# Down projection as seven block products with weight sums made on GpSimd, in a one-core decoder layer on Trainium2

## The chip, the core and the metric

The kernel is one launch on one of the eight cores of a Trainium2 chip. The metric is device time in microseconds (us), from launch to end, as the median of runs. Engines are named PE (TensorE), DVE (VectorE), ACT (ScalarE), POOL (GpSimd) and SP (SyncE, which here only issues DMAs).

## The reference, cut to what matters

The program computes one layer of a hybrid decoder: input projection, two kinds of attention over a prompt of 1024 tokens and 8 sampled tokens, output projection, and then a gated feed-forward part with a causal convolution of width 3. Only the last part is touched:

```python
h = _rmsnorm(x, pre_g)
g = h @ w_gate                    # (1032, 1024) @ (1024, 2816)
u = h @ w_up
gp = jnp.concatenate([prev.astype(g.dtype), g], axis=1)
c = conv_b
for j in range(CONV_W):
    c = c + conv_w[j] * gp[:, j:j + S]
a = jax.nn.gelu(c, approximate=True) * u
out = a @ w_down                  # (1032, 2816) @ (2816, 1024)
return x + _rmsnorm(out, post_g), gp[:, -(CONV_W - 1):]
```

## The kernel before

`TOK` = 1032 tokens (1024 + 8), `D` = 1024, `FF` = 2816 = `FC` = 22 blocks of `P` = 128. Every float32 operand of a product is split into a high part, written in the matmul's own format by ACT, and a low part (raw minus high) by DVE; a product is then three matmuls: high by high, high by low, low by high. Activations are kept transposed, features on the partitions and tokens along the free axis.

**Gate and up (`strassen`, blocks f = `PLAIN` = 3 to 21).** For each block of 128 gate and 128 up features, the product of a 2 x 2 split of the weights (gate or up, by two halves of the 1024 rows) with a 2 x 2 split of the tokens and rows (`HALF` = 516 tokens) is made from seven block products instead of eight. Each of the seven, `product(f, 0..6)`, is 4 x 3 x 2 = 24 matmuls of 258 tokens (`PART`), 168 in a block. Four sums of weight blocks (`sums`) are made by DVE as soon as the weights have landed. Results leave PSUM by ACT (`p1`, gate) and by DVE (`combine`: U2, U3, UP2, UP1, GATE2), and PE waits for several of these: product 3 for U2, product 5 for U3, product 6 for UP2. DVE's list in block f is: GATE2 of f-1, the four weight sums for f+1, the convolution of f-1 (one half), U2 of f, the other half of the convolution, one low part (1024 columns) for f+1, `multiply(f-1)` (the activation a of f-1 is then complete, in `cbuf`), the second low part (1536 columns), U3, the third low part (1024), UP2, UP1. Blocks 0 to 2 are made plainly, beside sums over tokens (`token_sums`) that DVE needs several long operations for.

SP's list in block f: wait for `multiply(f-1)`, store a (516 KB) to `a_dram`; wait for product 2, load the gate weights of block f+2 (512 KB); wait for product 5, load the up weights of f+2. POOL only copies ten columns of each gate block (`tail`).

**Down (`down(s)`, 88 steps).** The output (8 blocks d of 128 features, by 1032 tokens) is made in thirds of 344 tokens: sub-stages 0 and 1 (22 steps of 8 blocks), then the last third as 2 and 3 (22 steps of 4 blocks each). Each step loads a block row of `w_down` and, up to the last third, a third of a, splits both on ACT and DVE two steps ahead (`LAG`), and gives 3 matmuls of 344 tokens for each block. At the end of a sub-stage the banks are copied to `acc`. From step 46 on, tiles t of 128 tokens are turned on PE (`turn`), squared on ACT, given a root on POOL, scaled by DVE (`norm`), added to the residual by POOL (tiles below `EARLY` = 5) and stored. The remaining four tiles follow the last matmul; they use `scaled` columns and one DVE operation each.

What sets the order: every engine's list is written out by hand in one program order, and semaphores tie the lists together. The lines that the steps below use:

```python
def multiply(f):
    c = cbuf[:, f % 2, :]
    dve.wait_ge(gelu_done, f + 1)
    up_ready(dve, f)
    dve.tensor_tensor(c, c, ubuf[:, f % 2, :], ALU.mult).then_inc(mul_done, 1)
```

## Time and profile before

| | |
|---|---|
| runs | 1487.51 us median of 3 (1486.86 to 1490.24) |
| the profiled execution | 1485.53 us, its span 1483.8 us |
| PE busy | 1427.2 us (96%) |
| DVE, ACT, POOL busy | 865.6, 639.1, 365.8 us |
| gate and up by seven products, in the chain that ends last | 370.36 us of PE |
| down | 1211.9 to 1471.7 us |
| after the last matmul of down | 12.1 us |

The span is what the engines' records cover; 1.7 us of the execution lie outside it. PE runs without a gap from 841.5 us to the end of gate and up at 1211.9 us, and nearly so through down. A busy share of other engines says little here; what counts is when each link of a chain between them is done, compared with the time at which PE wants it. Those times are in the timeline rows further down.

### The profile page before, as it was taken

The numbers are of one execution on the slowest core, as the hardware profiler recorded it, in microseconds if no ns is written. First come the engines' busy times: TensorE is split into PE (matmuls) and PEld (weight loads), VectorE is DVE, ScalarE is ACT, GpSimd is POOL, SyncE is SP. The second block draws the span as 40 slices with busy tenths as digits, with TensorE's granted clock in tenths as the row PEclk, the third lists the DMA queues.
The fourth block names the chain that finished last, engine by engine and source line by source line (L and its number), as shares of the span: only waits on it lengthen the run. The fifth ranks groups of instructions, "written<-read, shape, count | busy, mean of one in ns | idle before, by whom it ended". The sixth has DMA issues, their size and how long they took to land. (4 is left out here: it accounts for less than half of the span.)

```text
span 1483.8 us, 26782 instructions
## 1 busy us (share of the span) xinstructions
PE 1427.2 (96%) x10372; PEld 1287.8 (87%) x10372; DVE 865.6 (58%) x1379; ACT 639.1 (43%) x1198; POOL 365.8 (25%) x549
## 2 busy tenths in 40 slices
PE   7999999999999899789999999999999999999998
PEld 6999777777777676477889999999999999999998
DVE  6422577667465555555439866766667755444674
ACT  6733555544455454433324523333233334433543
POOL 5223876756555541041100000000000000000120
PEclk9999999999999999999999999999999999999999
DMA  5113556777666564422321222222222246655773
GB/s 186 51 41 92 158 182 215 223 222 248 234 214 196 166 202 156 156 72 86 101 80 58 86 86 75 84 69 76 86 86 73 71 147 204 204 183 185 230 261 113
DMA packets 174840, 209.91 MB, mean 141 GB/s; under 512 B 22051, under 2 KB 118891, under 8 KB 174676
## 3 DMA queue, kind: packets, MB, share of 16 engines
q1 hardware_dynamic: 174714, 208.21, 44.5%
q8 instruction: 82, 1.34, 0.4%
q14 instruction: 44, 0.36, 0.1%
HBM read 178.37 MB, written 29.88 MB: 140 GB/s over the span
## 5 line engine op out<-in xcount | busy, mean ns | idle before, releaser
L632 POOL TENSOR_TENSOR k_page<-k_page,q_bc 128x256 f32<-128x256 f32 x256 | 183.4, 749 | 148.3 <-DMA k_page<-in_cache_fox_k 109.9
L1228 PE MATMUL PS<-ht_hi,w_hi 128*128 128x344 f32 x576 | 195.5, 339 | 6.7 <-POOL w_lo L602 4.7
L1228 PE MATMUL PS<-ht_hi,w_lo 128*128 128x344 f32 x576 | 186.4, 324 | 0.0
L1228 PE MATMUL PS<-ht_lo,w_hi 128*128 128x344 f32 x576 | 186.0, 323 | 0.0
L2466 PE MATMUL PS<-act_hi,wd_hi 128*128 128x344 f32 x528 | 169.0, 320 | 3.2 <-DVE act_lo L2301 3.2
L2466 PE MATMUL PS<-act_hi,wd_lo 128*128 128x344 f32 x528 | 168.6, 319 | 0.0
L2466 PE MATMUL PS<-act_lo,wd_hi 128*128 128x344 f32 x528 | 168.4, 319 | 0.0
L2298 DVE TENSOR_TENSOR wd_lo<-wd_raw,wd_hi 128x1024 fp32r<-128x1024 f32 (+1 forms) x88 | 87.8, 999 | 112.4 <-ACT act_hi L2109 92.4
L851 ACT ACTIVATE probs<-probs,stat 128x256 f32<-128x256 f32 (+7 forms) x128 | 98.5, 771 | 96.5 <-DVE stat L1101 95.9
L1228 PEld LDWEIGHTS PS<-ht_hi,w_hi 128*128 128x128 f32 x576 | 110.2, 191 | 32.7 <-issue 20.4
L2106 ACT ACTIVATE wd_hi<-wd_raw 128x1024 fp32r<-128x1024 f32 (+1 forms) x88 | 74.2, 845 | 139.9 <-DMA act_raw<-a_dram 103.7
L2421 PE MATMUL PS<-ht_hi,wgu_hi 128*128 128x258 f32 x608 | 122.6, 283 | 0.0
L2421 PE MATMUL PS<-ht_hi,wgu_lo 128*128 128x258 f32 x608 | 122.5, 283 | 0.0
L2421 PE MATMUL PS<-ht_lo,wgu_hi 128*128 128x258 f32 x608 | 122.5, 283 | 0.0
L2092 ACT ACTIVATE conv<-gate,conv_consts 128x1032 f32<-128x1032 f32 x22 | 27.6, 1254 | 207.4 <-DVE gate L2263 197.4
L2069 POOL COPY gate_tails<-gate 128x10 f32<-128x10 f32 x22 | 5.1, 230 | 438.2 <-DVE gate L2263 392.0
L1228 PEld LDWEIGHTS PS<-ht_lo,w_hi 128*128 128x128 f32 x576 | 110.2, 191 | 0.0
L1228 PEld LDWEIGHTS PS<-ht_hi,w_lo 128*128 128x128 f32 x576 | 110.0, 191 | 0.0
L2466 PEld LDWEIGHTS PS<-act_hi,wd_hi 128*128 128x128 f32 x528 | 99.2, 188 | 4.3 <-DVE act_lo L2301 4.2
L1025 DVE TENSOR_REDUCE scores<-k_page 128x16 f32<-128x1024 f32 x64 | 77.5, 1211 | 39.6 <-POOL k_page L632 39.4
L2466 PEld LDWEIGHTS PS<-act_lo,wd_hi 128*128 128x128 f32 x528 | 99.3, 188 | 0.0
L2466 PEld LDWEIGHTS PS<-act_hi,wd_lo 128*128 128x128 f32 x528 | 99.0, 188 | 0.0
(282 smaller groups left out, 3293.2 us busy)
## 6 DMA issues: line engine op xcount, KB each, us to landing
wd_raw<-in_w_down SPq DMA_DIRECT2D x44, 512.0 KB, 3.5
k_page<-in_cache_diff_k SPq DMA_DIRECT2D x64, 256.0 KB, 2.9
k_page<-in_cache_fox_k SPq DMA_DIRECT2D x64, 256.0 KB, 3.4
v_page<-in_cache_diff_v SPq DMA_DIRECT2D x64, 256.0 KB, 2.8
v_page<-in_cache_fox_v SPq DMA_DIRECT2D x64, 256.0 KB, 3.3
w_raw<-in_w_in SPq DMA_DIRECT2D x24, 512.0 KB, 4.9
a_dram<-conv SPq DMA_DIRECT2D x22, 516.0 KB, 3.1
act_raw<-a_dram SPq DMA_DIRECT2D x66, 172.0 KB, 3.7
```

The source lines that it names most:

```text
L632: ins = pool.tensor_tensor(kpage[:, g % 2, c:c + PIECE], kpage[:, g % 2, c:c + PIECE], qbc[:, c:c + PIECE], ALU.mult)
L851: act.activation(p, p, ACT.Exp, bias=stat[:, J % 8, m:m + 1], scale=-1.0, accum_out=stat[:, J % 8, 2 + m:3 + m]).then_inc(exp_done, 1)
L1025: dve.tensor_reduce(scores[:, b % 3, :, n, :], kpage[:, g % 2, :].rearrange("p (k m c) -> p k m c", k=2, c=HD), AX, ALU.add).then_inc(red_ ...
L1228: ins = pe.matmul(PS[:, z_bank(c), 0:THIRD], b[:, k, :], a[:, k, third(i)], start=(k == 0 and p == 0), stop=(k == KC - 1 and p == 2))
L2069: pool.tensor_copy(tails[:, f, :], gb[:, f % 2, SEQ:SEQ + DB + 2]).then_inc(tail_done, 1)
L2092: act.activation(cbuf[:, f % 2, :], gb[:, f % 2, 2:2 + TOK], ACT.Identity, bias=bias[:, f:f + 1], scale=taps[2][:, f:f + 1]).then_inc(c_in ...
L2106: act.activation(wd_hi[s % NW][:, c], wd_raw[s % NW][:, c], ACT.Copy).then_inc(down_high, 1)
L2298: dve.tensor_tensor(wd_lo[s % NW][:, c], wd_raw[s % NW][:, c], wd_hi[s % NW][:, c].bitcast(F32), ALU.subtract).then_inc(down_low, 1)
L2421: ins = pe.matmul(PS[:, bank + piece, 0:PART], w[:, k, :], a[:, k, piece * PART:(piece + 1) * PART], start=first and k == 0 and m == 0, st ...
L2466: ins = pe.matmul(PS[:, cell_bank(p, d), 0:THIRD], w[:, c], a[:, :], start=f == 0 and m == 0, stop=f == LAST and m == 2, skip_group_check= ...
```

## The change

The gate/up part keeps its products. The down product is now also made by a 2 x 2 split: 2 x 2 over (22 feature blocks in `NP` = 11 pairs) and (output features in halves of 512, tokens in halves of 516), with seven products in place of eight. `RUNS` = 9 runs of 11 steps: runs 0 to 4 are the products 0 to 4, a step being 4 output blocks x 3 x 2 = 24 matmuls of 258 tokens; products 5 and 6 are each made in two runs of half the tokens, 12 matmuls a step, so that the first tiles can be turned while the rest is still being made. Together 7 x 11 x 24 = 1848 matmuls.

The seven products need sums of operands. **Right sums** (of the activation a, four per pair of blocks): POOL makes them in `cbuf` after `multiply`, one behind even blocks and three behind odd ones, and SP stores seven halves (258 KB each, for 516 tokens) per pair to `b_dram`. **Weight sums** (`left_sums`): 44 chunks (256 KB), each a 128-column slice of four blocks of `w_down`. SP loads a chunk, POOL makes four dependent sums of 128 columns, SP stores the chunk to `s_dram`. Three chunks belong to each of blocks 4 to 17 and two to block 18, in two buffers. Down then loads whole left and right operands from `w_down`, `s_dram` and `b_dram`: 22 places for weights in place of 5, four for activations in place of 22. Finished products are added to the corners of the output by DVE as they leave PSUM; the fourth product is copied by ACT and added behind the first steps of run 4 (`add_fourth`). `EARLY` is 6, and POOL's residual add is cut in four.

```diff
+    NP = FC // 2
+    NW, NB = 22, 4
+    CHUNKS = 3
+    b_dram = nc.dram_tensor("b_dram", (7, NP, P, HALF), F32).ap()
+    s_dram = nc.dram_tensor("s_dram", (4, NP, P, WIDE), F32).ap()
+    chunks_of = lambda f: range(max(0, CHUNKS * (f - PLAIN - 1)), min(4 * NP, CHUNKS * max(0, f - PLAIN)))
...
+    FULL = 5
+    RUNS = FULL + 4
+    STEPS = RUNS * NP
+    LEFT = [(None, 0, 0), (0, 0, 0), (1, 0, 0), (3, 0, 0), (2, 0, 0), (None, 1, 1), (None, 1, 0)]
+    run_of = lambda s: s // NP
+    k_of = lambda s: s % NP
+    product_of = lambda r: r if r < FULL else FULL + (r - FULL) % 2
+    pieces_of = lambda r: (0, 1) if r < FULL else ((r - FULL) // 2,)
+    C11, C12, C21, C22 = range(4)
+    TARGET = [C11, C12, C21, C22, C12, C21, C11, C21, C11]
+    SOURCE = [None, C11, C12, C21, C12, C21, C11, C21, C11]
...
-                sp.dma_start(a_dram[f], cbuf[:, f % 2, :]).then_inc(a_stored[f % 2], 16)
+                if f % 2 == 0:
+                    store_half(f, 0, second_half)
+                else:
+                    store_half(f, 4, first_half)
+                    store_half(f, 6, second_half)
+
+            def store_sums(f):
+                k = f // 2
+                if f % 2 == 0:
+                    sp.wait_ge(pair_step, 4 * k + 1)
+                    store_half(f, 3, second_half)
+                else:
+                    sp.wait_ge(pair_step, 4 * k + 2)
+                    store_half(f - 1, 2, first_half)
+                    sp.wait_ge(pair_step, 4 * k + 3)
+                    store_half(f - 1, 1, second_half)
+
+            def store_last_sum(f):
+                sp.wait_ge(pair_step, 4 * (f // 2) + 4)
+                store_half(f, 5, second_half)
+
+            def load_chunk(c):
+                k, q = c // 4, c % 4
+                for i in range(2):
+                    src = io["w_down"][(2 * k + i) * P:(2 * k + i + 1) * P, :].rearrange("p (j c) -> p j c", j=2)[:, :, q * P:(q + 1) * P]
+                    sp.dma_start(chunk[c % CHUNKS % 2][:, 2 * i:2 * i + 2], src).then_inc(s_in, 16)
+
+            def store_chunk(c):
+                k, q = c // 4, c % 4
+                sp.wait_ge(sum_done, SUM_BASE + 4 * c + 4)
+                sp.dma_start(s_dram[:, k, :, q * P:(q + 1) * P].rearrange("m p c -> p m c"), chunk[c % CHUNKS % 2]).then_inc(s_stored, 16)
 
...
+                sums = chunks_of(f)
+                for c in sums[:2]:
+                    if c % CHUNKS == 0 and c:
+                        sp.wait_ge(s_stored, S_BASE + 16 * c)
+                    load_chunk(c)
                 if f:
-                    store_a(f - 1)
+                    store_act(f - 1)
                 if f + 2 < FC:
-                    for up in range(2):
-                        weights_free(sp, f, up)
-                        load_weights(sp, f + 2, up)
-            for s in range(2, STEPS):
+                    weights_free(sp, f, 0)
+                    load_weights(sp, f + 2, 0)
+                for c in sums[:1]:
+                    store_chunk(c)
+                if f:
+                    store_sums(f - 1)
+                for c in sums[2:]:
+                    sp.wait_ge(s_stored, S_BASE + 16 * (c - 1))
+                    load_chunk(c)
+                if f + 2 < FC:
+                    weights_free(sp, f, 1)
+                    load_weights(sp, f + 2, 1)
+                if f and f % 2 == 0:
+                    store_last_sum(f - 1)
+                for c in sums[1:]:
+                    store_chunk(c)
...
+            def left_sums(c):
+                a11, a21, a12, a22 = (chunk[c % CHUNKS % 2][:, m] for m in range(4))
+                n = SUM_BASE + 4 * c
+                pool.wait_ge(s_in, S_BASE + 32 * (c + (2, 1, 1)[c % CHUNKS]))
+                pool.tensor_tensor(a22, a21, a22, ALU.add).then_inc(sum_done, 1)
+                pool.wait_ge(sum_done, n + 1)
+                pool.tensor_tensor(a21, a11, a21, ALU.subtract).then_inc(sum_done, 1)
+                pool.wait_ge(sum_done, n + 2)
+                pool.tensor_tensor(a11, a22, a11, ALU.subtract).then_inc(sum_done, 1)
+                pool.wait_ge(sum_done, n + 3)
+                pool.tensor_tensor(a12, a12, a11, ALU.subtract).then_inc(sum_done, 1)
+            def right_sums(f):
+                k = f // 2
+                pool.wait_ge(mul_done, f + 1)
+                b11, b12, b21, b22 = cbuf[:, 0, second_half], cbuf[:, 0, first_half], cbuf[:, 1, second_half], cbuf[:, 1, first_half]
+                if f % 2 == 0:
+                    pool.wait_ge(a_stored[0], 16 * (4 * k + 1))
+                    pool.tensor_tensor(b11, b12, b11, ALU.subtract).then_inc(pair_step, 1)
+                else:
+                    pool.tensor_tensor(b12, b22, b12, ALU.subtract).then_inc(pair_step, 1)
+                    pool.wait_ge(a_stored[0], 16 * (4 * k + 2))
+                    pool.tensor_tensor(b11, b22, b11, ALU.subtract).then_inc(pair_step, 1)
+                    pool.wait_ge(pair_step, 4 * k + 3)
+                    pool.wait_ge(a_stored[1], 16 * (3 * k + 2))
+                    pool.tensor_tensor(b21, b11, b21, ALU.subtract).then_inc(pair_step, 1)
             for f in range(FC):
+                for c in chunks_of(f):
+                    left_sums(c)
                 tail(f)
+                right_sums(f)
...
-                    pool.tensor_tensor(out[:, u % OS, :], out[:, u % OS, :], xr[:, u % OS, :], ALU.add).then_inc(out_early, 1)
+                    for part in range(4):
+                        c = slice(part * D // 4, (part + 1) * D // 4)
+                        pool.tensor_tensor(out[:, u % OS, c], out[:, u % OS, c], xr[:, u % OS, c], ALU.add).then_inc(out_early, 1)
...
                 if f >= 2:
-                    act.wait_ge(a_stored[f % 2], 16 * (f // 2))
+                    act.wait_ge(a_stored[f % 2], 16 * (4, 3)[f % 2] * (f // 2))
+                    act.wait_ge(pair_step, 4 * (f // 2))
...
+                if s == NP:
+                    evacuate_first()
+                if s == 4 * NP:
+                    evacuate_fourth()
...
+            def evacuate(r):
+                pieces = pieces_of(r)
+                for d in range(4):
+                    src = PS[:, bank_of(r, d):bank_of(r, d) + len(pieces), 0:PART]
+                    if r == 0:
+                        if d % 2 == 0:
+                            cell_ready(dve, r, d)
+                            dve.tensor_copy(corner(C11, d), src).then_inc(cell_dve, 1)
+                        continue
+                    cell_free(dve, r - 1, d)
+                    if r == 4:
+                        dve.wait_ge(cell_dve, 10 + 2 * d + 2)
+                    cell_ready(dve, r, d)
+                    dst = corner(TARGET[r], d, pieces)
+                    if product_of(r) == 5:
+                        dve.tensor_tensor(dst, dst, src, ALU.subtract).then_inc(cell_dve, 1)
+                    else:
+                        dve.tensor_tensor(dst, corner(SOURCE[r], d, pieces), src, ALU.add).then_inc(cell_dve, 1)
+
+            def add_fourth(d):
+                p5, u3, u4 = corner(C22, d), corner(C21, d), corner(C12, d)
+                dve.wait_ge(cell_act, 2 + d + 1)
+                dve.wait_ge(cell_dve, 6 + d + 1)
+                dve.tensor_tensor(u4, u4, p5, ALU.add).then_inc(cell_dve, 1)
+                dve.wait_ge(cell_dve, 10 + 2 * d + 1)
+                dve.tensor_tensor(p5, p5, u3, ALU.add).then_inc(cell_dve, 1)
...
+                if s >= NP and run_of(s) != 4 and k_of(s) == (0 if run_of(s) < FULL else 1):
+                    evacuate(run_of(s) - 1)
+                if 4 * NP < s <= 4 * NP + 4:
+                    add_fourth(k_of(s) - 1)
+                if s >= STEPS - 4:
+                    scale(4 + s - (STEPS - 4))
...
+                for d in range(4):
+                    if k == 0:
+                        if r == 0 and d:
+                            if d == 1:
+                                pe.wait_ge(act_done, 2 * (FC - PLAIN))
+                            else:
+                                pe.wait_ge(evac_done, evacs(FC - 1, (UP1, GATE2)[d - 2]))
+                        elif r == FULL:
+                            cell_free(pe, r - 1, 1 + d // 2)
+                        elif r:
+                            cell_free(pe, r - 1, d)
+                    first = c.start
+                    for m, (w, a) in enumerate(((w_hi2[n % NW], b_hi[slot]), (w_hi2[n % NW], b_lo[slot]), (w_lo2[n % NW], b_hi[slot]))):
+                        for piece in range(len(pieces_of(r))):
+                            ins = pe.matmul(PS[:, bank_of(r, d) + piece, 0:PART], w[:, d * P:(d + 1) * P],
+                                            a[:, first + piece * PART:first + (piece + 1) * PART],
+                                            start=k == 0 and m == 0, stop=k == LAST and m == 2, skip_group_check=True)
+                    if k == LAST or d == 3:
                         ins.then_inc(down_done, 1)
```

SP, around block 6 of gate and up (`wgu_raw` is a set of gate and up weights, `conv` holds the activation a, `wd_sums` is a chunk; e_mul_done is raised by `multiply`, a_lf_in0 by POOL's weight sums, a_v_in0 by a chunk's landed store, e_pair_step by right sums). Before:

```order
L1506 DMA wgu_raw_94_10955<-in_w_gate 128x8x128 [waits e_prod_done]
L1506 DMA wgu_raw_94_10955<-in_w_up 128x8x128 [waits e_prod_done]
L2002 DMA a_dram<-conv_103_12174 128x1032 [waits e_mul_done]
L1506 DMA wgu_raw_91_10952<-in_w_gate 128x8x128 [waits e_prod_done]
L1506 DMA wgu_raw_91_10952<-in_w_up 128x8x128 [waits e_prod_done]
```

And now:

```order
L2083 DMA wd_sums_188_12259<-in_w_down 128x2x128 x2
L2054 DMA b_dram<-conv_103_12174 128x516 [waits e_mul_done]
L1507 DMA wgu_raw_94_10955<-in_w_gate 128x8x128 [waits e_prod_done]
L2088 DMA s_dram<-wd_sums_187_12258 128x4x128 [waits a_lf_in0]
L2054 DMA b_dram<-conv_103_12174 128x516 [waits e_pair_step]
L2083 DMA wd_sums_187_12258<-in_w_down 128x2x128 [waits a_v_in0]
L2083 DMA wd_sums_187_12258<-in_w_down 128x2x128
L1507 DMA wgu_raw_94_10955<-in_w_up 128x8x128 [waits e_prod_done]
L2088 DMA s_dram<-wd_sums_188_12259 128x4x128 [waits a_lf_in0]
```

Between the load of the gate weights and that of the up weights SP now stands at three other waits: for POOL's weight sums, for its right sums and for the landing of a chunk's store.

POOL in the same place. Before, it has the copies of `tail` alone (the first three in the plain blocks):

```order
L2063 MEMSET stat_12168 128x16
L2065 MEMSET gate_12173 128x2 x2
L2069 COPY gate_tails_12167<-gate_12173 128x10 [waits e_plain_evac] x3
L2069 COPY gate_tails_12167<-gate_12173 128x10 [waits e_evac_done,e_act_done] x19
L2076 TENSOR_SCALAR stat_12168<-stat_12168 128x1 [waits e_y_sq]
```

And now, for block 3's activation and the first chunk (the second and third chunk read the same):

```order
L2184 COPY gate_tails_12167<-gate_12173 128x10 [waits e_evac_done,e_act_done]
L2206 TENSOR_TENSOR conv_12174<-conv_12174 128x516 [waits e_mul_done]
L2208 TENSOR_TENSOR conv_12174<-conv_12174 128x516 [waits e_a_stored0]
L2211 TENSOR_TENSOR conv_12174<-conv_12174 128x516 [waits e_a_stored1,e_pair_step]
L2190 TENSOR_TENSOR wd_sums_12258<-wd_sums_12258 128x128 [waits a_kp_in0]
L2192 TENSOR_TENSOR wd_sums_12258<-wd_sums_12258 128x128 [waits a_lf_in0]
L2194 TENSOR_TENSOR wd_sums_12258<-wd_sums_12258 128x128 [waits a_lf_in0]
L2196 TENSOR_TENSOR wd_sums_12258<-wd_sums_12258 128x128 [waits a_lf_in0]
```

A block's chunks stand behind the right sums of the block before, which wait for that block's `multiply`.

DVE at the end of the first long stretch of down, where a bank group is emptied. Before, between sub-stages 0 and 1:

```order
L2298 TENSOR_TENSOR wd_lo_12188<-wd_raw_12193,wd_hi_12183 128x1024
L2301 TENSOR_TENSOR act_lo_12218<-act_raw_12240,act_hi_12196 128x344
L2309 COPY acc_12261<-PS 128x344 x4
L2298 TENSOR_TENSOR wd_lo_12189<-wd_raw_12194,wd_hi_12184 128x1024
L2301 TENSOR_TENSOR act_lo_12219<-act_raw_12241,act_hi_12197 128x344
```

And now, between run 4 and run 5:

```order
L2459 TENSOR_TENSOR wd_lo_12213<-wd_raw_12235,wd_hi_12191 128x512
L2460 TENSOR_TENSOR act_lo_12250<-act_raw_12254,act_hi_12246 128x258
L2459 TENSOR_TENSOR wd_lo_12214<-wd_raw_12236,wd_hi_12192 128x512
L2460 TENSOR_TENSOR act_lo_12250<-act_raw_12254,act_hi_12246 128x258
L2479 TENSOR_TENSOR acc_12260<-acc_12260,PS 128x516 x4
L2459 TENSOR_TENSOR wd_lo_12215<-wd_raw_12237,wd_hi_12193 128x512
```

The four additions of a finished product stand where copies stood, behind the low parts of the second step of the new run.

## Rows read from the trace of the kernel before

**Rows 1.** Chain that ended last, in order of time: start us, us, what.
```profile
841.55 370.36 PE PS L2421 x3072
1211.92 167.78 PE PS L2466 x1068
...
1385.24 0.87 PE PS L2483 x8
```

**Rows 2.** Busy time by stretch: down, and what follows (columns: us, PE, PEld, DVE, ACT, POOL, PEclk, DMA, GB/s).
```profile
1211.90:1471.70 259.80, 256.55 (x1647) 254.57 (x1645) 134.60 (x184) 111.18 (x180) 17.29 (x16) 1.00 0.62 203
1471.70:1483.80 12.10, 7.35 (x65) 6.51 (x64) 6.78 (x9) 4.47 (x9) 2.94 (x8) 0.92 0.34 133
```

**Rows 3.** Timeline of DVE in one gate/up block: start us, us, what, [idle before].
```profile
1010.42 0.70 DVE L2212 TENSOR_TENSOR wgu_raw<-wgu_raw 128x512 f32<-128x512 f32 x1 [0.17 <-DMA wgu_raw<-in_w_up]
...
1015.35 0.69 DVE L2263 TENSOR_TENSOR u<-PS,p 128x516 f32<-128x516 f32 x1 [0.71 <-PE PS L2421]
...
1018.50 1.23 DVE L2244 TENSOR_TENSOR conv<-conv,up 128x1032 f32<-128x1032 f32 x1
1019.65 1.75 DVE L1515 TENSOR_TENSOR wgu_lo<-wgu_raw,wgu_hi 128x1536 fp32r<-128x1536 f32 x1
1021.32 0.69 DVE L2263 TENSOR_TENSOR u<-PS,p 128x516 f32<-128x516 f32 x1
1021.93 1.22 DVE L1515 TENSOR_TENSOR wgu_lo<-wgu_raw,wgu_hi 128x1024 fp32r<-128x1024 f32 x1
1024.02 0.70 DVE L2263 TENSOR_TENSOR up<-PS,u 128x516 f32<-128x516 f32 x1 [0.87 <-PE PS L2421]
```

**Rows 4.** Timeline of SP's DMA queue in the same block.
```profile
1019.76 0.34 SPq L2002 DMA_DIRECT2D a_dram<-conv  x1
1020.15 0.44 SPq L1506 DMA_DIRECT2D wgu_raw<-in_w_gate  x1
1026.91 0.37 SPq L1506 DMA_DIRECT2D wgu_raw<-in_w_up  x1
```

**Rows 5.** DMA issues of the whole run: count, KB each, median us to landing.
```profile
a_dram<-conv SPq DMA_DIRECT2D x22, 516.0 KB, 3.1
wgu_raw<-in_w_gate SPq DMA_DIRECT2D x22, 512.0 KB, 4.6
wgu_raw<-in_w_up SPq DMA_DIRECT2D x22, 512.0 KB, 3.8
...
out_o_dk<-k_rows SPq DMA_DIRECT2D x8, 256.0 KB, 3.2
...
out_o_fk<-k_rows SPq DMA_DIRECT2D x8, 256.0 KB, 2.4
```

**Rows 6.** Groups of POOL by form: count, busy us, mean ns, idle before.
```profile
L632 POOL TENSOR_TENSOR k_page<-k_page,q_bc 128x256 f32<-128x256 f32 x256 | 183.4, 749 | 148.3 <-DMA k_page<-in_cache_fox_k 109.9 <-DMA q_bc<-qs_dram 34.4 <-PE PS L1354 4.0
...
L643 POOL TENSOR_TENSOR lf_after<-lf_four 128x56 f32<-128x56 f32 x8 | 2.4, 303 | 0.6
```

**Rows 7.** Timelines of POOL and DVE, a residual add in down.
```profile
1391.79 2.41 POOL L2083 TENSOR_TENSOR out_rows<-out_rows,x_rows 128x1024 f32<-128x1024 f32 x1 [3.62 <-DVE out_rows L2327]
...
1392.50 2.24 DVE L2298 TENSOR_TENSOR wd_lo<-wd_raw,wd_hi 128x512 fp32r<-128x512 f32 x1 [0.80 <-ACT act_hi L2109]
...
1395.09 0.68 DVE L2298 TENSOR_TENSOR wd_lo<-wd_raw,wd_hi 128x512 fp32r<-128x512 f32 x1
```

**Rows 8.** Timeline of DVE between the plain blocks and block 3.
```profile
819.49 6.74 DVE L2293 TENSOR_TENSOR t_lo<-t_raw,t_hi 128x2064 fp32r<-128x2064 f32 x3
...
834.46 0.69 DVE L2263 TENSOR_TENSOR u<-PS,p 128x516 f32<-128x516 f32 x1
```

**Rows 9.** Groups of DVE by form, in down: count, busy us, mean ns, idle before.
```profile
L2298 DVE TENSOR_TENSOR wd_lo<-wd_raw,wd_hi 128x512 fp32r<-128x512 f32 x44 | 33.9, 774 | 36.4 <-ACT wd_hi L2106 19.8 <-ACT act_hi L2109 16.4
```

**Rows 10.** Busy time by stretch around a pause of PE at 640 us.
```profile
640.00:642.20 2.20, 0.35 (x2) 0.14 (x2) 0.89 (x2) 0.91 (x3) 0.14 (x1) 1.00 0.00 0
642.20:645.40 3.20, 3.17 (x8) 2.52 (x9) 2.26 (x2) 3.20 (x4) 3.20 (x3) 0.50 0.72 175
```

More of the change, by code:

```diff
@@ L1943, in ffn, with right_free @@
+    def right_free(eng, s):
+        h = s - FULL * NP
+        if NB <= s < FULL * NP:
+            step_ready(eng, s - NB)
+        elif 0 <= h < 2 * NB:
+            step_ready(eng, min(FULL * NP - 3 + h // 2, FULL * NP - 1))
+        elif h >= 2 * NB:
+            step_ready(eng, s - 2 * NB)
+    ends_of = lambda s: 4 if k_of(s) == LAST else 1
     steps_done = lambda s: sum(ends_of(n) for n in range(s + 1))
-    loads_of = lambda s: 32 if s < 3 * FC else 16
-    down_loads = lambda s: sum(loads_of(n) for n in range(s % NW, s + 1, NW))
@@ L1959, in ffn @@
-    PAIR = [6, 4, 6, 4, 6, 4, 6, 0, 2]
+    PAIR = [6, 4, 6, 4, 6, 4, 6, 4, 6]
+    SCALED_PAIR = {6: 0, 7: 2, 8: 4}
     y_of = lambda t: PS[0:rows(t), PAIR[t]:PAIR[t] + 2, :].rearrange("p b c -> p (b c)")
-    EARLY = sum(third_of(t) < 2 for t in range(NS))
-    TAIL_STEP = 2 * FC + 1
-    turn_step = lambda t: TAIL_STEP + 2 + 4 * t
+    scaled_y = lambda t: PS[0:rows(t), SCALED_PAIR[t]:SCALED_PAIR[t] + 2, :].rearrange("p b c -> p (b c)")
+    EARLY = 6
+    TAIL_STEP = FULL * NP + 1
+    turn_step = lambda t: TAIL_STEP + (1, 8, 13, 18, 24, 30)[t]
@@ L2152, in _ @@
                 else:
[L2153 removed]
+                    high_parts(0)
                 if f:
@@ L2196, in _ @@
                         squares(t)
-            evacuate(3)
+            for d in range(2):
+                scale(d)
             for t in range(EARLY, NS):
@@ L2389, in _ @@
                         norm(t)
-            evacuate(3)
-            scale(3)
+            evacuate(RUNS - 1)
+            for d in range(2, 4):
+                scale(d)
             for t in range(EARLY, NS):
```

300 lines of the change are left out of this document (159 added, 141 removed).

## Prediction

> **What bounds the kernel now.** I read the chain that ended last first. From 841.55 to 1211.92 us it is nothing but gate/up matmuls, 370.36 us for 3072 of them, and then down matmuls, 167.78 us for 1068 [rows 1]. The table by stretch says the same of down: PE is busy for 256.55 of 259.80 us [rows 2]. So PE sets the end here, and fewer matmul columns are worth their full time, as long as nothing new makes PE wait. The pitch of a matmul is 370.36/3072 = 0.1206 us at 258 tokens and 167.78/1068 = 0.1571 us at 344. Next I read one gate/up block on DVE and SP [rows 3, 4], for what must be ready when. A block is 168 x 0.1206 = 20.25 us. Call M the end of `multiply`, 1018.50 + 1.23 = 1019.73. The up weights are asked for 7.2 us behind M (1026.91), when product 5 is done, and DVE's weight sums start as they land: in this block at 1010.42, 0.17 us after DVE was free. So that load has no slack against DVE already now. From the first weight sum to M are 9.3 us, of which 0.71 are a wait for PE, so 8.6 of work in a row. DVE's slack against PE is small: U3 is ready at 1022.0, and PE could use it when product 4 ends, shortly before 1024.0. That is 1.9 us.
>
> **Down, matmuls.** 22 x 24 x 3 = 1584 matmuls at 0.1571 are 248.8 us. Seven products are 1848 at 0.1206, 222.9 us: **-26.0**. The pitch is that of the same form in gate/up, also with two pieces on one weight block. Six tiles and half of two more are turned before the last matmul, in place of five: 16 more transposes at 0.87/8 [rows 1], +1.7. The stretch after the last matmul, 12.1 us [rows 2], loses half of its turns and one tile: -2.
> **Down, new waits.** A full step of DVE is a low part of 512 (0.68 undisturbed [rows 7]; the mean of 44 is 0.77 [rows 9]) and one of 516 (0.69), 1.4 of PE's 2.9 us. In runs 5 and 6 a step is 12 x 0.1206 = 1.45 us, and DVE has 0.68 + 0.4 (half of 0.69, with a start) = 1.1, beside additions of 0.69 and one 1.28 us norm a tile. That is nearly full, and GpSimd's cut adds each hold it for up to 0.75. I put +1 there. Between runs 4 and 5 the additions stand behind two low parts, and PE's first step needs two of them: +2. The fourth product's copies and additions: +1; the later run ends +1. Transfers are 24 matmuls of 520 KB, 180 GB/s, against 203 now [rows 2]; I charge nothing, and up to +5 if they land late. PE's 3.2 us of idle in down now go half. Sum for down: -26.0 + 1.7 - 2 + 5 - 1.6 = **-23** (-27 to -16).
>
> **Gate/up, the loop through SP.** Here the change adds waits. SP loads the up weights of block f+2 only behind (a) GpSimd's first weight sums of block f, (b) the right sums, (c) the landing of the first chunk's store. GpSimd's list puts (a) behind the right sums of f-1, and these wait for M. The next M waits for the up weights. That is a closed loop, once per block: M, right sums, weight sums, store, loads, DVE, next M. Queued behind SP's wait are the up weights; behind those stands DVE, and behind DVE's U2 and U3 stands PE.
>
> Prices. A GpSimd sum of 516 columns is not in the trace: 256 columns take 0.75 [rows 6], 1024 take 2.41 [rows 7], so 2.16 ns a column and 1.31 us; one of 128 is 0.47 (56 columns take 0.30 [rows 6]), with 0.08 between dependent ones, so a chunk is 2.2 us. A 256 KB store lands in 2.4 to 3.2 us, 516 KB in 3.1; I take 3.0, and 2.7 for the single half. Loads of 512 KB take 3.8 alone and 4.6 close behind another transfer [rows 5]; I take 4.25. Each issue costs 0.4.
>
> DVE and GpSimd get in each other's way: at 1392.50 a DVE low part of 512 columns, 0.68 otherwise, took 2.24 us and ended 0.5 us after GpSimd's add (1391.79 + 2.41) did [rows 7]. I take it that two such operations never run together. *The Trainium skill, "SBUF — State Buffer", "SBUF: two separate sides", says that a DVE operation with two SBUF inputs and a GpSimd operation that reads SBUF exclude one another, and the loser fully blocks; the trace agrees (2.24 for 0.68). By that rule the sum is the one below; without it, it is the first rival.* Beside M DVE runs its 1.75 low part until M+1.65, and a 1.22 one behind U3.
>
> - Even f (three right sums): first sum M+1.65 to 2.95; DVE's 1.22 part to 4.1; two more sums and a semaphore to 6.75; chunk to 8.95; store landed 12.0; two chunk loads and the up load issued by 12.9; landed 17.2; then 8.6 and 0.4 for meeting the third chunk's sums: next M at **26.2**.
> - Odd f (one right sum): its store landed 2.7, DVE's 1.22 part until 3.5, sum to 4.8, chunk 7.0, store 10.1, loads 11.0, landed 15.3: next M at **24.3**.
>
> Mean 25.25, against PE's 20.25: 5.0 us a block in iterations 4 to 17, 14 x 5.0 = 70; +2.5 for iteration 18 (two chunks, no third to wait for); -1.9 for the slack that is used once: **+71**. Nearest bounds: all stages at their short ends (stores 2.4, load 3.8, no collisions) give 21.4 a block, +16; stores 3.2, load 4.6 and a lost turn at the port in each block give 27, +95.
>
> **Gate/up, entry.** Between the plain blocks and block 3 DVE runs without idle (6.74 us of `t_lo` at 819.49, and U2 at 834.46 starts with no wait [rows 8]). The four right sums of the first pair push in between: 4 x 1.31 = **+5** (0 to +7). In blocks 19 to 21 nothing is added that PE would see: the right sums end at M+7, and the load waits for product 5 anyway.
>
> **Sum.** -23 + 71 + 5 = +53. Against the profiled execution 1485.5 + 53 = 1538.5; the median of the runs is 2.0 above that execution, so 1487.5 + 53 = **1540.5**.
>
> **Rivals.**
> 1. *The loop holds, the collisions cost nothing* (GpSimd and DVE mostly miss each other). Loop 23.9 and 23.3, +3.4 a block, 14 x 3.4 - 1.9 + 5 - 23 = +28: 1515. For it: outside M, DVE is idle much of a block. Against: right sums are released at M, where two low parts stand. 0.20.
> 2. *Faster.* Stores and loads at their short ends, and M reached earlier: the loop fits under PE's block. Place: SP's up load. It decides at 20.25 - 8.6 = 11.6 us from M to landed up weights; I count 15.3 to 17.2, the short ends 12.8. Gain 23 less the entry: 1470; with a loop of 21.4: 1484. For it: five blocks without chunks and loose orders elsewhere. Against: (c) alone is 2.4 to 3.2. 0.12.
> 3. *Slower still*: loop 27 or more, as twice the traffic of now lengthens every landing, or PE's clock: after 2.2 us with 0.35 busy it was granted 0.50, the 1.2 GHz level, for 3.2 us [rows 10]. The waits for U2 would be 3 to 5 us each. Half clock adds 1.6 us a block; I count it as hidden, since PE then waits for U2 again. *"TensorE: Matmul & The Clock Gate" of the Trainium skill, "HAM oscillation — how this bites in real kernels", has each tile start cold behind such a wait; here that is this 1.6 us.* If not hidden, 14 x 1.6 = +22: 1562; with the long loop 1565 to 1590. 0.15.
> 4. *No change*: a loop of 21.7 pays the gain back exactly. 0.03.
>
> **Chances.** Forecast 0.50, rivals 0.20, 0.12, 0.15, 0.03. Faster by over 0.2% (about what a measurement of this kernel can tell from no change) 0.12, within 0.03, slower 0.85. The range must take in rival 1 and the lower part of rival 3: 1500 to 1572 holds 0.5 + 0.17 + 0.12, about 8 in 10.
>
> **What would show it.** Right: blocks of about 25 us from block 5 on, alternating by about 2; DVE idle before the first weight sum, ended by the up weights, some 5 us a block; SP's issue of the up load 11 to 13 us behind M; GpSimd's 516-column sums at M stretched beyond 1.31; down 23 us shorter. Wrong: blocks of 20.25 with the up load issued at product 5, or a pitch in down above 0.1206, or DVE low parts ending late in runs 5 and 6 by more than a few us.

## The result and the profile after

The changed kernel takes 1540.57 us (median of 4 runs, 1535.76 to 1541.27), beside 1488.74 us before (4 runs, 1486.86 to 1490.24). The ratio is 1.033, 95% interval 1.031 to 1.036: slower. The profiled execution has a span of 1538.1 us.

I lay the profile of after beside that of before in four stretches. The marks are the issue of the load of `ffn_pre_g`, which no edit here moves (642.4 before, 649.8 after), the loads of `w_up` on SP's queue, the first matmul of down, and the end.

| stretch | before | after | difference | forecast |
|---|---|---|---|---|
| start to `ffn_pre_g` | 642.4 | 649.8 | +7.4 | 0 |
| second to sixth load of `w_up` (entry) | 73.40 | 77.07 | +3.7 | +5 |
| sixth to 20th (14 blocks) | 283.4 | 346.38 | +63.0 | +70 |
| 20th to the first matmul of down | 83.8 | 85.7 | +1.9 | +0.6 |
| down and tail | 271.9 | 250.2 | -21.7 | -23 |

The first line is code that the change leaves alone. In the 14 profiles of this study that mark stood between 642.4 and 650.6 us, and before happened to be the earliest. So inside the marks behind it the change moved this execution by +46.9, where I had forecast +53. The timed medians differ by 51.8. There is one profile of before, so whether its first stretch is always the shorter one is open.

SP's queue in one block, after (start us, us, what), which answers [rows 4]. M, the end of `multiply`, was at 1017.18:

```profile
1017.21 0.81 SPq L2054 DMA_DIRECT2D b_dram<-conv  x2
1018.07 0.45 SPq L1507 DMA_DIRECT2D wgu_raw<-in_w_gate  x1
1025.69 0.37 SPq L2088 DMA_DIRECT2D s_dram<-wd_sums  x1
1026.10 1.00 SPq L2054 DMA_DIRECT2D b_dram<-conv  x2
1028.03 1.21 SPq L2083 DMA_DIRECT2D wd_sums<-in_w_down  x2
1029.28 0.61 SPq L1507 DMA_DIRECT2D wgu_raw<-in_w_up  x1
```

GpSimd and DVE in the same block; the last line is the next M:

```profile
1017.26 2.74 POOL L2206 TENSOR_TENSOR conv<-conv 128x516 f32<-128x516 f32 x1 [8.88 <-DVE conv L2403]
1019.97 2.28 POOL L2208 TENSOR_TENSOR conv<-conv 128x516 f32<-128x516 f32 x1
1022.32 1.30 POOL L2211 TENSOR_TENSOR conv<-conv 128x516 f32<-128x516 f32 x1
...
1017.10 1.75 DVE L1516 TENSOR_TENSOR wgu_lo<-wgu_raw,wgu_hi 128x1536 fp32r<-128x1536 f32 x1
...
1019.37 1.71 DVE L1516 TENSOR_TENSOR wgu_lo<-wgu_raw,wgu_hi 128x1024 fp32r<-128x1024 f32 x1
...
1033.81 0.69 DVE L2371 TENSOR_TENSOR wgu_raw<-wgu_raw 128x512 f32<-128x512 f32 x1 [7.52 <-DMA wgu_raw<-in_w_up]
...
1041.08 1.23 DVE L2403 TENSOR_TENSOR conv<-conv,up 128x1032 f32<-128x1032 f32 x1
```

The load of the up weights is issued 12.1 us behind M, where it was 7.2 before. DVE stands idle for 7.52 us, ended by its landing, and reaches the next M 25.1 us after the last. SP's store of M goes out 0.03 us behind it in every block, so SP itself is never late here. In the block behind it, with one right sum, the load is issued at 1052.61 and M follows at 1065.81, 23.5 us after 1042.31. The waits of 820 to 1290 us say the same in sum (us, times, longest):

```profile
POOL conv L2204 <- DMA b_dram<-conv: 129.9, 10, 18.2
ACT conv L2240 <- DMA b_dram<-conv: 112.4, 8, 14.9
...
DVE wgu_raw L2371 <- DMA wgu_raw<-in_w_up: 96.2, 17, 8.8
...
PEld PS L2598 <- DVE u L2422: 47.1, 17, 5.2
```

Down, and what follows the last matmul (us, PE busy, PEld, DVE, ACT, POOL, PEclk, DMA, GB/s), which answer [rows 2]:

```profile
1287.90:1528.00 240.10, 233.90 (x1926) 231.59 (x1925) 139.87 (x225) 102.78 (x198) 32.27 (x40) 0.99 0.66 202
1528.00:1538.10 10.10, 4.56 (x40) 3.96 (x40) 4.80 (x7) 3.73 (x7) 2.21 (x6) 0.99 0.28 107
...
1445.00:1505.00 60.00, 55.01 (x445) 53.34 (x443) 41.34 (x69) 29.09 (x66) 22.95 (x30) 0.97 0.70 225
```

### The profile page after: what moved, and what is told of

It is laid out like the page before. It is cut to its first block and busy times, and to the rows that moved or that the text cites. A ratio compares the mean times of both kernels' runs of the same rounds, so it can differ in the third digit from the quotient of the medians.

```text
span 1538.1 us, 27932 instructions
## 1 busy us (share of the span) xinstructions
PE 1426.1 (93%) x10628; PEld 1279.1 (83%) x10628; DVE 875.0 (57%) x1417; ACT 633.3 (41%) x1216; POOL 543.5 (35%) x788
## 5 line engine op out<-in xcount | busy, mean ns | idle before, releaser
L2650 PE MATMUL PS<-act_hi,wd_hi 128*128 128x258 f32 x616 | 140.6, 286 | 6.2 <-DVE acc L2479 3.3
L2598 PE MATMUL PS<-t_hi,wgu_hi 128*128 128x258 f32 x456 | 99.3, 301 | 43.8 <-DVE u L2422 43.6
L2650 PE MATMUL PS<-act_lo,wd_hi 128*128 128x258 f32 x616 | 138.7, 283 | 0.0
L2650 PE MATMUL PS<-act_hi,wd_lo 128*128 128x258 f32 x616 | 138.6, 283 | 0.0
L2598 PEld LDWEIGHTS PS<-t_hi,wgu_hi 128*128 128x128 f32 x456 | 74.8, 200 | 48.8 <-DVE u L2422 47.1
L1513 ACT ACTIVATE wgu_hi<-wgu_raw 128x1024 fp32r<-128x1024 f32 (+1 forms) x63 | 72.2, 1182 | 84.7 <-DMA wgu_raw<-in_w_up 48.4
L2459 DVE TENSOR_TENSOR wd_lo<-wd_raw,wd_hi 128x512 fp32r<-128x512 f32 x77 | 56.1, 728 | 80.4 <-ACT act_hi L2258 80.4
```

Source lines behind the costliest of these rows:

```text
L1513: act.activation(hi[f % 2][:, a:b], part(raw, f, a, b), ACT.Copy).then_inc(gu_hi, 1)
L2459: dve.tensor_tensor(w_lo2[n % NW][:, :], w_raw2[n % NW][:, :], w_hi2[n % NW][:, :].bitcast(F32), ALU.subtract).then_inc(down_low, 1)
L2598: ins = pe.matmul(PS[:, bank + piece, 0:PART], w[:, k, :], a[:, k, piece * PART:(piece + 1) * PART], start=first and k == 0 and m == 0, st ...
L2650: ins = pe.matmul(PS[:, bank_of(r, d) + piece, 0:PART], w[:, d * P:(d + 1) * P], a[:, first + piece * PART:first + (piece + 1) * PART], st ...
```

## The experiments

The theory to be tested: a gate/up block is as long as the loop from M over right sums, chunk sums, landing and loads to the up weights and the next M. Its rival: GpSimd's work beside VectorE and the doubled traffic make blocks long by themselves. In the edits SP's list of one iteration is written in short; `right sums` is `store_sums(f - 1)`, `c0` to `c2` are the block's chunks. What each kernel gave (the timed ratio is to before on the same chip; the last three columns are from the profiles: second to sixth load of `w_up`, which the expectations also call third to sixth or seventh; mean of the 14 blocks behind them; start of down's first matmul to the end, which is 0.1 to 0.2 us more than by the chain's piece above). Before itself had a median of 1490.4 beside e1 to e5, 1490.8 beside e7 and e8, 1492.4 beside e9 and e10, 1490.5 beside e11 to e13 and 1485.0 in one run beside e14:

| kernel | us | ratio (95%) | entry | block | down |
|---|---|---|---|---|---|
| before | 1488.7 | | 73.4 | 20.24 | 272.0 |
| after | 1540.6 | 1.033 (1.031 to 1.036) | 77.1 | 24.74 | 250.4 |
| e1 up load before the landing | 1534.8 | 1.030 (1.025 to 1.035) | 77.3 | 24.30 | 250.4 |
| e2 up load before all of the chunks | 1525.9 | 1.024 (1.021 to 1.027) | 77.3 | 24.13 | 250.7 |
| e4 no chunks | 1465.8, one run | | 78.8 | 20.24 | 246.0 |
| e5 small right sums | 1516.9, one run | | 76.1 | 23.61 | 252.2 |
| e7 e2, two chunks a block | 1476.1 | 0.991 (0.989 to 0.994) | 82.2 | 20.24 | 251.2 |
| e8 e2, chunk loads behind M | 1492.7 | 1.002 (1.000 to 1.004) | 79.1 | 21.86 | 250.6 |
| e9 e7, later stores of y | 1475.8 | 0.991 (0.988 to 0.993) | 82.6 | 20.24 | 244.6 |
| e10 e9, chunks spread | 1487.6 | 0.997 (0.995 to 0.999) | 83.3 | 20.76 | 251.7 |
| e11 two chunks, order of after | 1530.6 | 1.028 (1.026 to 1.031) | 96.2 | 22.78 | 248.6 |
| e12 e7 again | 1476.5 | 0.990 (0.989 to 0.992) | 83.0 | 20.24 | 251.4 |
| e13 e9 again | 1475.7 | 0.990 (0.988 to 0.991) | 82.8 | 20.24 | 247.9 |
| e14 e7, no chunks in blocks 0 to 2 | 1472.7, one run | | 78.9 | 20.24 | 248.9 |

**e1: the up load one step earlier.**

```diff
 store_chunk(c0)
 store_sums(f - 1)
+weights_free(sp, f, 1); load_weights(sp, f + 2, 1)
 wait for the landing of c0; load_chunk(c2)
-weights_free(sp, f, 1); load_weights(sp, f + 2, 1)
```

> The load of w_up stands one step earlier on SyncE: behind the store of the first chunk and the stores of the right sums, ahead of the wait for that store's landing. Theory (the loop M, right sums, chunk sums, landing, loads, up weights, next M sets the block): the load is issued some 2.2 us sooner in a block with three right sums (M+9.9 for M+12.1) and 2.7 us sooner in the other (M+7.6 for M+10.3), so the blocks take 22.9 and 20.6 us for 25.1 and 23.3, and the kernel 1540.5 - 14 x 2.45 = about 1506 us (1500 to 1512). Rival (the blocks are long because GpSimd and VectorE slow each other and the chunk transfers load the DMA engines, whatever the order of issue): no more than 5 us, 1535 to 1541.

Measured: 1534.8 us, blocks of 24.30. Most of the saving did not come. In one block M was at 1011.19 and the load was issued at 1022.43, M+11.2 and not M+9.9; in the next, M 1036.17, it went out at 1044.78, M+8.6 and not M+7.6. In both SP was itself late: it was issuing chunk loads until 1011.71 and 1036.69, half a microsecond behind M. In the second the half of M landed later for it, and the right sum, which waits for that, started at M+4.3 in place of M+3.4. Over the blocks of e1 SP's store of M was 0.6 to 2.5 us late. That pointed at the chunk chain as a loop of its own.

**e2: nothing of the chunks ahead of the up load.**

```diff
+store_sums(f - 1)
+weights_free(sp, f, 1); load_weights(sp, f + 2, 1)
 store_chunk(c0)
-store_sums(f - 1)
 wait for the landing of c0; load_chunk(c2)
-weights_free(sp, f, 1); load_weights(sp, f + 2, 1)
```

> SyncE's order in a block becomes: store of the right sums, load of w_up, store of the first chunk, landing, the rest. Theory: nothing of the chunks is ahead of the load of w_up any more; it is issued when PE's product frees its buffer (M+7.2 in the kernel before), the block is PE's 20.25 us again, and the 65 us that the loop cost in gate/up go: 1476 us (1473 to 1482), which is also faster than the kernel before. Rival (collisions and traffic, whatever the order): 1530 to 1541. If the loop goes but the right sums in VectorE's way cost 1 to 2 us in a block, 1490 to 1505.

Measured: 1525.9 us, blocks of 24.13. From one issue of the up load to the next it is mostly near 21 and near 28 us by turns, and from M to M 22.2 to 26.2. My theory said 20.25, and its number fell. SP's queue of e2, where M was at 1009.60:

```profile
1002.37 6.54 SPq L2088 DMA_DIRECT2D s_dram<-wd_sums  x2
1010.83 2.52 SPq L2083 DMA_DIRECT2D wd_sums<-in_w_down  x4
1013.39 1.08 SPq L2054 DMA_DIRECT2D b_dram<-conv  x2
1014.52 0.46 SPq L1507 DMA_DIRECT2D wgu_raw<-in_w_gate  x1
1015.02 1.45 SPq L2054 DMA_DIRECT2D b_dram<-conv  x2
1016.51 0.49 SPq L1507 DMA_DIRECT2D wgu_raw<-in_w_up  x1
1021.27 0.37 SPq L2088 DMA_DIRECT2D s_dram<-wd_sums  x1
1025.98 1.21 SPq L2083 DMA_DIRECT2D wd_sums<-in_w_down  x2
1027.24 0.60 SPq L2054 DMA_DIRECT2D b_dram<-conv  x1
1027.88 5.82 SPq L2088 DMA_DIRECT2D s_dram<-wd_sums  x2
1035.64 2.52 SPq L2083 DMA_DIRECT2D wd_sums<-in_w_down  x4
1038.20 0.60 SPq L2054 DMA_DIRECT2D b_dram<-conv  x1
```

The up load is issued at M+6.9, as expected (in the next block, with M at 1034.40, only at M+9.4). But two things are new. SP stands in the chunk chain until 1010.83 and then issues four chunk loads of 0.6 us each, so the store of M goes out 3.8 us late. And all transfers now go out in one burst: from 1010.83 to 1016.51, 2.6 MB, and the up weights, last of them, start DVE only at 1025.32, 8.8 us after their issue:

```profile
1025.32 0.69 DVE L2371 TENSOR_TENSOR wgu_raw<-wgu_raw 128x512 f32<-128x512 f32 x1 [5.69 <-DMA wgu_raw<-in_w_up]
```

The chunk chain is a second closed loop: M, its store, right sums, c0's sums, store, landing, c2's load and sums, store, landing, four loads, and only then SP's store of the next M. Once around, from the store of one M (1013.39) to the store of the next (1038.20), it takes 24.8 us, and that is the length of this block from M to M (24.80), where PE needs 20.25. SP's store is 3.8 to 7.1 us late in all but the first block with chunks. The two loops are not apart in e2: SP's lateness also puts the up load at the end of the burst. They are told apart below, by e11 and e10.

**e4 and e5: one half of GpSimd's work taken out.** e4 drops the chunks:

```diff
-for c in chunks_of(f): left_sums(c)
-sums = chunks_of(f)
+sums = ()
```

It also stores the first right sum of an odd block one sum later, and reads `w_down` in place of `s_dram`. e5 keeps the order and cuts the right sums:

```diff
-b11, b12, b21, b22 = cbuf[:, 0, second_half], cbuf[:, 0, first_half], ...
+b11, b12, b21, b22 = cbuf[:, 0, HALF:HALF + 8], cbuf[:, 0, 0:8], ...
```

> The chunks' loads, sums and stores are left out (the down-projection reads plain blocks of w_down in their place); the right sums on GpSimd and everything else stay. Theory: the right sums alone cost the block nothing, since without the chunk stores the load of w_up waits for nothing behind M+7.2: 1472 to 1480 us. Rival (the right sums beside VectorE's low parts lengthen the block): 1490 or more.

> The four right sums of a pair are done on 8 columns in place of 516; chunks and order stay. Theory: the loop keeps the landing of the stores of M (3.2 us, for which the first or the last of the sums waits), the chunk sums 2.1, the landing 2.4 and the loads 1.3, so the load of w_up is issued at M+9.1 in both blocks and a block takes 22.2 us: 1540.5 - 14 x 2.0 - 2 = about 1510 us (1503 to 1515). Rival (it is the right sums' collision with VectorE that makes the block long): back to 20.25 us a block, 1476.

Measured: e4 1465.8 us, below even its expected range, with blocks of 20.24; e5 1516.9, a little over its range, with blocks of 23.61 for 22.2: behind one sum the up load went out at M+9.1 to 9.6, about as forecast (9.1), but behind three at M+9.9 to 11.7, and it landed 4.5 to 7.0 us later. So the right sums alone cost a block nothing, and with hardly any right sums and the chunks in place most of the loss stays. The collision at M is thus not what makes the block long: of the 4.5 us that a block of after is longer, 3.4 are still there without it. Part of the entry is told as well. Its last step, fifth to sixth load, is 18.51 us before, 21.27 after, 21.33 in e4 and 18.50 in e5: 2.8 us there belong to the right sums. Its first step, second to third load, was 9.5 before, and it varies between kernels whose code is the same up to there (10.6 after, 12.3 and 12.4 in e4 and e5); no run shows why.

**e7 and e8: the chunk chain shortened, or SP brought to M on time.** Both have e2's order. e7:

```diff
-CHUNKS = 3
+CHUNKS = 2
-chunks_of = lambda f: range(max(0, CHUNKS * (f - PLAIN - 1)), min(...))
+chunks_of = lambda f: range(CHUNKS * f, CHUNKS * f + CHUNKS)
```

e8 moves a step in SP's list:

```diff
-wait for all chunk stores; load_chunk(c0); load_chunk(c1)
 store_act(f - 1)
 weights_free(sp, f, 0); load_weights(sp, f + 2, 0)
+wait for all chunk stores; load_chunk(c0); load_chunk(c1)
 store_sums(f - 1)
```

> SyncE's order of e2, and the 44 chunks spread over all 22 blocks, two in each (before: three in each of blocks 4 to 17 and two in block 18), so that no chunk waits in mid-block for a landing. Theory (after e2: a block is the longer of two loops, the one through the load of w_up and the one of the chunk chain, which SyncE's next store of M stands behind): the chunk chain now ends 13.5 us behind M and its four loads are issued by M+16, well ahead of the next M; the load of w_up goes out at M+7.2 and lands 4.5 to 5 us later, so blocks of 20.25 to 20.9 us, and 1 to 4 us for the sums in the first blocks: 1475 to 1490 us. Rival (what lengthens the blocks is the amount of GpSimd work and traffic, which is the same in sum): still over 1515.

> SyncE's order of e2 with three chunks a block, but the wait for the last block's chunk stores and the first four chunk loads stand behind the store of M and the load of w_gate, no longer ahead of them. Theory: SyncE reaches the store of M on time (in e2 it came 3.8 to 4.4 us late), but the chunk chain, M, right sums, c0 sums at M+8.7, store, landing, load of c2 landed at M+17.5, its sums to M+20 or 21, is still as long as a block: 21 to 22.5 us a block, 1485 to 1505 us. If the chain were of no weight once SyncE is on time, 1476; if lateness were not the point, 1526 as e2.

Measured: e7 1476.1 us, faster than before by 0.9% (0.6 to 1.1%); e8 1492.7 us, blocks of 21.86. Both totals are within what was expected. Not as expected are e7's entry, 4.9 us longer than e2's for 1 to 4, and e8's SP: it was on time in four of the 14 blocks and over 2.6 us late in six, so e8 shortens the second loop and does not do away with it. In e7 SP's queue is at rest before M (1012.06):

```profile
1006.31 2.52 SPq L2083 DMA_DIRECT2D wd_sums<-in_w_down  x4
1012.09 0.34 SPq L2054 DMA_DIRECT2D b_dram<-conv  x1
1012.47 0.43 SPq L1507 DMA_DIRECT2D wgu_raw<-in_w_gate  x1
1016.66 0.33 SPq L2054 DMA_DIRECT2D b_dram<-conv  x1
1019.23 0.37 SPq L1507 DMA_DIRECT2D wgu_raw<-in_w_up  x1
```

The up load is out at M+7.2 and starts DVE 4.2 us later (1023.40). PE never stops, with GpSimd busy for 60 of 160 us and DMA at 147 GB/s, against 84 in the same stretch before:

```profile
1040.00:1200.00 160.00, 160.00 (x1331) 160.00 (x1330) 113.45 (x136) 53.43 (x56) 59.65 (x86) 1.00 0.49 147
```

GpSimd's sums at M are as stretched as in after (2.75 and 2.29 us for 1.30), and it costs nothing. Traffic and collisions by themselves are not what made the block long; inside a loop they still lengthen its links, as the landings of the up load show (median 4.5 us in after, 4.1 in e7, 3.8 before).

**e11: the spread of e7 with the order of after.**

> SyncE's order of the changed kernel, untouched, with the 44 chunks spread over 22 blocks as in e7: it differs from e7 in the order alone, and from the changed kernel in the spread alone. Theory: no wait for a landing is left ahead of the load of w_up, but the first chunk's store is, so the load is issued at M+10.1 behind three right sums and M+7.6 behind one and lands 4.5 us later, 8.6 us ahead of the next M: blocks of 23.2 and 20.7 us, mean 21.9, which is 1.7 us a block over e7 in 16 blocks: 1476 + 27 = 1503 us (1496 to 1510). Rival (with the chain short enough the order is of no weight): 1476. Rival (the order is all, the spread nothing): 1540.

Measured: 1530.6 us. It shows that the order counts too, but my number was 28 us low. This is the first loop by itself: SP's chunk loads are out 3 us or more before each M and its store of M is on time in every block, and still a block takes 22.78. In the blocks the loop is as expected up to the issue (M 1018.73, load 1028.69, M+10.0; M 1042.61, load 1050.27, M+7.7); the landing took 4.7 to 5.1 us behind one right sum and 5.4 to 7.7 behind three, where I had 4.5, and that makes the block 22.78 for 21.9, some 12 us in all. Another 14 are the entry, 96.2 us against 82.2 in e7. Between 785 and 798 us VectorE has no idle time, and GpSimd's chunk sums take five times their length, as e7's profile shows too:

```profile
788.43 2.41 POOL L2196 TENSOR_TENSOR wd_sums<-wd_sums 128x128 f32<-128x128 f32 x1
790.80 2.53 POOL L2190 TENSOR_TENSOR wd_sums<-wd_sums 128x128 f32<-128x128 f32 x1
...
795.53 2.45 DVE L2439 TENSOR_TENSOR t_raw<-t_raw,ht_lo 128x2064 f32<-128x2064 f32 x1
```

Behind such sums SP's up load has to wait in e11, and not in e7. In e11's entry it follows the first chunk's store each time, here behind chunk sums of 2.5 and 2.4 us:

```profile
842.90 0.37 SPq L2088 DMA_DIRECT2D s_dram<-wd_sums  x1
...
844.36 0.56 SPq L1507 DMA_DIRECT2D wgu_raw<-in_w_up  x1
```

**e9, e10, e12, e13: what is left in down and at the entry.** In e7's half runs SP's loads of right halves stand behind the store of an output tile, which waits for GpSimd's residual sums (SP's queue; 5.7 us pass between the first two lines):

```profile
1412.09 0.38 SPq L2051 DMA_DIRECT2D act_raw<-b_dram  x1
1417.81 0.34 SPq L2098 DMA_DIRECT2D out_y<-out_rows  x1
1418.20 0.43 SPq L2093 DMA_DIRECT2D x_rows<-x_dram  x1
1418.73 0.73 SPq L2051 DMA_DIRECT2D act_raw<-b_dram  x1
```

e9 and e10:

```diff
-if t < EARLY and s == turn_step(t) + 10:
+if t < EARLY and s == min(turn_step(t) + 13, STEPS - 1):     # e9, e10
+CHUNK_COUNT = [0 if f in (3, 4) else 3 if f in (7, 11, 15, 19) else 2 for f in range(FC)]     # e10
```

> As e7, but SyncE's stores of the first six output tiles, which wait for GpSimd's residual sums, stand three half steps (4.3 us) later in its list (the last of them at the last step). Theory: in e7 the loads of the right halves queue behind such a wait (1412.5 to 1417.8), land late, PE stands still for 2.3 us at 1424 and is then granted 0.88 of its clock until 1440 (1.7 us), and again 1.8 us in the stretch before: 2 to 5 us come back, 1471 to 1475 us. Rival (these stalls are the transfers' own duration of 5.6 us at a DMA share of 0.67 to 0.84): 1475 to 1478 us.

> As e9, but no chunks in blocks 3 and 4, where VectorE has no idle time and chunk sums of 0.46 us took 2.4, and a third chunk in blocks 7, 11, 15 and 19, which follow a block with one right sum. Theory: e7 lost 8.7 us against the kernel before between the third and the sixth load of w_up (before: 73.4 us, e7: 82.2) where the changed kernel lost 3.7; some 4 to 5 us come back, and each of the four blocks with a third chunk costs 0 to 1.5: 1 to 5 us under e9. Rival (the first two blocks' chunks are what costs there): as e9, or 1 to 3 us over it.

> The kernel of e7 once more, beside that of e9 on one chip: 1476 us (1472 to 1480), its down-projection 251 us from the first matmul to the end.

> The kernel of e9 once more, beside that of e7. In their profiles e9's down-projection took 244.6 us and e7's 251.2, but e10, with e9's edit in it, took 251.7. If the later stores of y are worth what the profile of e9 shows, 4 to 6 us under e12 here and a down-projection of 245 us; if that profile was a lucky one, within 2 us of e12.

Measured: e9's profile has down in 244.6 us, 6.6 less than e7's, but its timed runs are no faster: 1475.8 beside 1476.1, and on one chip 1475.7 (e13, 4 runs, 1473.7 to 1476.5) beside 1476.5 (e12, 5 runs, 1473.9 to 1482.7), with 247.9 and 251.4 in down. So of the two answers that e13 had left open it is the second, a profile in which down happened to be short. Down varies between 246.0 (e4) and 252.2 (e5) without this edit, and it took 251.7 in e10 with it. No run shows that the later stores are worth anything. e10's expectation failed: the entry stayed at 83.3 us without chunks in blocks 3 and 4, and the four blocks with a third chunk cost 8 us together (14 x 0.52, and 1.1 behind the 20th load). What they cost shows the second loop by itself. The up load stands ahead of all chunks, and with two chunks SP's store of M is on time; in the three of the 14 blocks that follow a third chunk it is 2.7, 4.6 and 7.1 us late, the up load lands 6.4 to 7.4 us behind its issue, and the block takes 21.8, 23.5 and 26.1 us. For the last of these M was at 1119.44:

```profile
1124.02 2.51 SPq L2085 DMA_DIRECT2D wd_sums<-in_w_down  x4
1126.58 1.07 SPq L2056 DMA_DIRECT2D b_dram<-conv  x2
```

**e14: the first three blocks without chunks.**

```diff
-chunks_of = lambda f: range(CHUNKS * f, CHUNKS * f + CHUNKS)
+chunks_of = lambda f: range(CHUNKS * f, CHUNKS * f + CHUNKS) if f >= 3 else ()
```

> As e7, but the six chunks of blocks 0 to 2 are left out (the first two left blocks of a product are read as plain blocks of w_down), so that their loads, sums and stores are gone from the first three blocks, and blocks 3 and 4 keep theirs. e7 took 82.2 us from the third to the seventh load of w_up, e2 in the same order with its first chunks in block 5 took 77.3, and e10 without chunks in blocks 3 and 4 83.3. If it is the chunks of blocks 0 to 2 that cost there: 77 to 79 us, and the kernel 1470 to 1473 us. If it is any chunk before block 5: 80 or more, and 1474 or more.

Measured: entry 78.9 us, 1472.7 us. So 3.3 of the 8.8 us that e7 loses at the entry come from the six chunks of blocks 0 to 2. The rest is what e4 has too (78.8), which has no chunks at all, so the chunks of blocks 3 and 4 cost nothing that shows. The gain is read from the marks; the one timed run beside one of before gives 0.992, no less than e7's 0.991. Where they could be done instead, without a third chunk in later blocks, was not tried.

## Why the prediction was right, point by point

**The total** came out at 1540.6 for 1540.5, and that is closer than the working deserves. Its parts sum to +53; in the profile they are +46.9, and 7.4 us of unchanged stages, in which this profile of before was the shortest of 14, fill the gap. That is luck. The two parts that carry the sum were also too large with opposite signs: the loop by 7 us, the gain in down by 1.3.

**Matmuls of down: right.** PE's first 264 matmuls take 31.81 us, 0.1205 each, and another 768 take 92.72, 0.1207 each:

```profile
1287.89 31.81 PE PS L2650 x264
...
1322.74 92.72 PE PS L2650 x768
```

Times 1848 that is 222.7 to 223.1 us for the forecast 222.9, a pitch read from another stage of the same form. The stretch behind the last matmul is 10.1 us for 12.1 [rows 2], -2.0 as forecast. PE's idle before the last matmul is 6.2 us against 3.25, +3.0 where the sum had +3.4 (its +5 less 1.6). The places were partly others: borders (waits for `acc`, 3.9 us in all) and late right halves (2.2 us and more), where I had put the first on one border and for the second charged nothing. With +1.7 for the turns these are -26.1 + 1.7 - 2.0 + 3.0 = -23.4. Down and tail gave -21.7. The missing 1.7 is probably the clock behind pauses: from 1445 to 1505 us, where PE was busy for 55.0 of 60 us, 0.97 was granted, and 0.03 x 60 is 1.8, an estimate that no run tests.

**The loop: right in its links and their order, with sizes off both ways.** Forecast and measured behind M, in the block with three right sums: sums done 6.75 and 6.4; first chunk 8.95 and 8.5; its store landed 12.0 and 10.8; up load issued before 12.9 and at 12.1; landed 17.2 and 16.6; next M 26.2 and 25.1. With one right sum: sum done 4.8 and 4.7, chunk 7.0 and 6.7, landed 10.1 and 9.05, up load issued before 11.0 and at 10.3, landed 15.3 and 15.0, next M 24.3 and 23.5. The term most off is the landing of the 256 KB store: 3.0 by the nearest rows [rows 5], 2.3 here (1025.69 to 1028.03), 0.7 us in each block. From the landed up weights to M it was 8.5 for 9.0, as the 0.4 for VectorE meeting the third chunk's sums did not show, and the sums were 0.3 to 0.4 shorter. Against that, the two chunk loads took 0.6 us each to issue for 0.4, and the up load landed in 4.5 and 4.7 us for 4.25. These two blocks average 24.3 for the forecast 25.25; the 14 have 24.74 (25.8 and 23.65 of each kind), because the up load took 4.4 to 5.8 us there, 4.85 in the mean. So the error of -0.5 a block is what is left of larger ones that partly cancel.

**The collision: right as a size, and of less weight than I gave it.** The first right sum ended at M+2.8 for M+2.95; the second overlaps a low part of 1.22 us that took 1.71. *The Trainium skill, "SBUF — State Buffer", "SBUF: two separate sides", has the two engines shut each other out; the trace agrees: GpSimd's 2.74 is the 1.75 of DVE's operation, less 0.16 of start, and about 1.2 of its own.* Rival 1 took the collisions out and came to 1515; e5 takes nearly all of GpSimd's part in them out, and the sums with it, and came to 1516.9, with blocks of 23.61. That the two times agree says nothing, as they take out different things. Sums and collisions together are worth 1.1 us a block in the loop of after. Outside a loop, in e4 and e7, they cost a block nothing.

**The entry: +5 forecast, +3.7 measured**, of which e4 and e5 give 2.8 to the right sums of the first pair. The rest lies in the step from the second to the third load and has no cause shown.

**The clock: hidden, as assumed.** PE's pause of 3.76 us ahead of product 3 is followed by 3.2 us at a granted 0.54, nearly all at the 1.2 GHz level (after, last columns PEclk, DMA, GB/s):

```profile
1037.20:1040.00 2.80, 1.33 (x9) 1.33 (x10) 2.80 (x6) 1.96 (x3) 0.00 (x0) 0.92 0.62 182
1040.00:1043.20 3.20, 3.20 (x18) 3.20 (x18) 3.20 (x3) 1.53 (x2) 0.00 (x0) 0.54 0.02 8
```

It did not lengthen the block: from the landed up weights at 1033.81 to M at 1042.31 DVE works without a wait for PE, and SP's next up load waits for the landing of the chunk's store, not for PE.

**What the prediction did not see** is the second loop. I counted SP's steps ahead of the up load and not those behind it, which return to SP's store of the next M. In after they fit: the last chunk loads of that block were out at 1038.45, 3.9 us ahead of the next M. The store of M was on time in every block. So the second loop cost nothing there, and the total does not show the omission. It had a part in e1 (SP 0.6 to 2.5 us late) and decided e2, where I expected 1506 and 1476 and measured 1534.8 and 1525.9. Rival 2, the faster kernel at 1470 to 1484, was the right number for a kernel without either loop: 1476.1 in e7.
